# Gate table, gate waits and the order of weight splits in a two-block transformer kernel

## What is computed

```python
# linear attention's gates: two rank-16 projections, log-sigmoid, running sums
la_f = heads(jax.nn.log_sigmoid((zf @ w_gate_f + b_gate_f).astype(F32)) / GLA_TAU, GLA_HK)
la_b = heads(jax.nn.log_sigmoid((zb @ w_gate_b + b_gate_b).astype(F32)) / GLA_TAU, GLA_HK)
b = jnp.cumsum(log_a.astype(F32).reshape(bsz, nh, n, c, dk), axis=3)
q_in = qf * jnp.exp(b)
scores = jnp.einsum('bhncd,bhnjd->bhncj', q_in, kf * jnp.exp(-b))
# differential attention: queries and keys normed and turned by rope, then scores
q, k, v = split_cols(h @ w_in, [D_MODEL, D_MODEL, D_MODEL])
q = rope(rms_norm(q.reshape(bsz, seq, nh, 2, dh), g_q).reshape(bsz, seq, 2 * nh, dh), pos)
k = rope(rms_norm(k.reshape(bsz, seq, nh, 2, dh), g_k).reshape(bsz, seq, 2 * nh, dh), pos)
s = jnp.einsum('bhtqd,bhtkd->bhtqk', q_blk, kt).astype(F32) * scale
# the gated addition at the end of each layer
gate = jax.nn.sigmoid(rms_norm(h, ple_norm[i]) @ ple_w_gate[i])
h = h + gate * (p[i] @ ple_w_proj[i])
```

## Time and profile before

| | us |
|---|---|
| median of three runs (899.43 to 899.6) | 899.53 |
| the profiled execution | 899.7 |
| its span | 897.9 |
| TensorE busy | 892.8 |
| VectorE busy | 653.1 |
| ScalarE busy | 506.9 |
| fetches of units | 295 of 512 KB |

### The profile page before, as it was taken

The page is one execution under the profiler, slowest core; times in us unless marked ns, Lnnn a source line. Parts: engine busy times, 40 slices in busy tenths (PEclk is TensorE's granted clock), DMA queues, the critical chain, the costliest instruction groups (busy, mean ns, idle before and its releaser), DMA issues.

```text
span 897.9 us, 12240 instructions
## 1 busy us (share of the span) xinstructions
PE 892.8 (99%) x4364; PEld 738.6 (82%) x4364; DVE 653.1 (73%) x985; ACT 506.9 (56%) x820; POOL 69.4 (8%) x88
## 2 busy tenths in 40 slices
PE   9999999999999999999999999999999999999998
PEld 8988888888888888778888888888888888887777
DVE  5985478777745688997787777645778997779763
ACT  6756455444444666788664444434665555577681
POOL 0000100000000303211000000000010000215100
PEclk9999999999999999999999999999999999999999
DMA  7674558867755656434387766746567876566621
GB/s 258 205 236 136 179 186 293 283 235 240 247 202 187 226 187 221 143 116 141 127 277 268 244 243 237 253 137 235 197 244 239 286 248 211 191 212 226 222 87 47
DMA packets 76988, 187.47 MB, mean 209 GB/s; under 512 B 6852, under 2 KB 31812, under 8 KB 76936
## 3 DMA queue, kind: packets, MB, share of 16 engines
q1 hardware_dynamic: 75480, 182.99, 59.9%
q0 software_dynamic: 1024, 3.15, 1.0%
q10 hardware_dynamic: 432, 0.66, 0.2%
HBM read 171.83 MB, written 14.94 MB: 208 GB/s over the span
## 4 chain that ended last, share of the span: by engine, by line
PE 98%; DMA 1%; DVE 1%; ACT 0%; issue 0%; DVEq 0%; ACTq 0%
PE bank L1818 86%; PE bank L1856 3%; PE bank L1871 1%; PE bank L2131 1%; PE bank L2157 1%; PE bank L2241 1%; PE bank L2271 1%; DMA h_land<-gate_blocks 1%; PE bank L2142 0%; PE bank L1914 0%; PE bank L1978 0%; PE bank L2227 0%; PE bank L2026 0%; PE bank L2030 0%; PE bank L2251 0%; PE bank L2117 0%
## 5 line engine op out<-in xcount | busy, mean ns | idle before, releaser
L699 ACT ACTIVATE whi<-raw 128x1024 fp32r<-128x1024 f32 x295 | 306.3, 1060 | 181.2 <-DMA raw<-stream_dram 106.2
L1108 DVE TENSOR_TENSOR wlo<-raw,whi 128x1024 fp32r<-128x1024 f32 x295 | 347.9, 1214 | 57.1 <-ACT whi L699 56.7
L1818 PE MATMUL bank<-whi,x_hi 128*128 128x512 f32 x560 | 152.5, 394 | 0.0
L1818 PE MATMUL bank<-wlo,x_hi 128*128 128x512 f32 x560 | 149.9, 390 | 0.0
L1818 PE MATMUL bank<-whi,x_lo 128*128 128x512 f32 x560 | 149.8, 389 | 0.0
L1818 PEld LDWEIGHTS bank<-wlo,x_hi 128*128 128x128 f32 x560 | 105.2, 188 | 22.1
L1818 PEld LDWEIGHTS bank<-whi,x_lo 128*128 128x128 f32 x560 | 105.2, 188 | 21.9
L1818 PEld LDWEIGHTS bank<-whi,x_hi 128*128 128x128 f32 x560 | 103.6, 188 | 22.1 <-issue 1.8
L1818 PE MATMUL bank<-whi,y_hi 128*128 128x512 f32 x396 | 107.8, 394 | 0.6 <-ACT ple_gate L895 0.5
L1818 PE MATMUL bank<-wlo,y_hi 128*128 128x512 f32 x396 | 106.0, 390 | 0.0
L1818 PE MATMUL bank<-whi,y_lo 128*128 128x512 f32 x396 | 106.0, 390 | 0.0
(11 more groups left out here) (252 smaller groups left out, 898.7 us busy)
## 6 DMA issues: line engine op xcount, KB each, us to landing
raw<-stream_dram SPq DMA_DIRECT2D x295, 512.0 KB, 4.6
ffn_blocks<-ffn_blk SPq DMA_DIRECT2D x22, 256.0 KB, 2.0
ffn_land<-ffn_blocks SPq DMA_DIRECT2D x22, 256.0 KB, 4.0
second_blocks<-h_blk SPq DMA_DIRECT2D x8, 256.0 KB, 2.0
h_land<-second_blocks SPq DMA_DIRECT2D x8, 256.0 KB, 2.8
cv_blocks<-cv_blk SPq DMA_DIRECT2D x7, 256.0 KB, 5.0
cv_land<-cv_blocks SPq DMA_DIRECT2D x7, 256.0 KB, 3.1
h_blocks<-h_blk SPq DMA_DIRECT2D x3, 512.0 KB, 6.3
```

Source lines behind the costliest of these rows:

```text
L699: A(whi[:, u % RING, :], raw[:, u % RAW, :], ACT.Copy).then_inc(sem("w_hi"), 1)
L1108: V.tensor_tensor(wlo[:, u % RING, :], raw[:, u % RAW, :], whi[:, u % RING, :].bitcast(F32), ALU.subtract).then_inc(sem("w_lo"), 1)
L1818: last = T.matmul(bank[pair + t][:, :], lhs[a][:, kt, t * P:(t + 1) * P], w[:, u % RING, kk * NW:(kk + 1) * NW], start=part != 1 and k == ...
```

## The change

It has three parts. At each layer's gate, ScalarE takes the sigmoid of one column into a buffer that nobody reads, right behind the squares and ahead of the wait for `rstd`, which loads sigmoid's table there. VectorE waits for the sigmoids of one half of the tokens ahead of each multiplication, where it waited for both ahead of the first. And the tables of order are renumbered: linear attention's `gates` on VectorE go from unit 5 to 4 and `expabs` on ScalarE from 6 to 5; differential attention's first two tiles on ScalarE go from units 4 and 8 to 2 and 6, and VectorE's steps for them two units or one earlier.

```diff
     "act": (
-        (6, "expabs", 0), (7, "ln", 0), (9, "cumulate", 0), (10, "cumulate", 1), (13, "tile", 3), (17, "cross", 0),
+        (5, "expabs", 0), (7, "ln", 0), (9, "cumulate", 0), (10, "cumulate", 1), (13, "tile", 3), (17, "cross", 0),
...
     "dve": (
-        (4, "zT", 0), (4, "tile", 1), (5, "z4", 0), (5, "gates", 0), (7, "ln", 0), (9, "tile", 2),
+        (4, "zT", 0), (4, "tile", 1), (5, "z4", 0), (4, "gates", 0), (7, "ln", 0), (9, "tile", 2),
...
     "act": (
-        (4, "tile", 0), (8, "tile", 1), (11, "qkT", 0), (12, "qkT", 1), (12, "tile", 2), (12, "qkT", 2),
+        (2, "tile", 0), (6, "tile", 1), (11, "qkT", 0), (12, "qkT", 1), (12, "tile", 2), (12, "qkT", 2),
...
     "dve": (
-        (5, "rope", 0), (6, "more", 0), (6, "sums", 0), (8, "rope", 1), (8, "sums", 1), (10, "more", 1),
+        (3, "rope", 0), (4, "more", 0), (4, "sums", 0), (7, "rope", 1), (7, "sums", 1), (10, "more", 1),
...
-        sb("rstd_q", [P, TT])
+        spare = sb("spare", [P, TT])
...
                 squares(j, 1)
+                A(spare[:, n:n + 1], cols[:, 0:1], ACT.Sigmoid)
                 act.wait_ge(sem("rstd"), j + 1)
...
-                    dve.wait_ge(sem("ple_sig"), TT * (2 * n + half + 1))
                     c.wait(dve, "w_used", END[t + 2])
                     for k in range(TT):
+                        dve.wait_ge(sem("ple_sig"), TT * (2 * n + half) + k + 1)
                         V.tensor_tensor(gated[:, k, :], sig[:, k, :], bank[2 * ((t + 1) % 2) + k][:, :], ALU.mult)\
                             .then_inc(sem("ple_gated"), 1)
```

## The result

The changed kernel takes 901.64 us (median of 18 runs, 900.56 to 902.46), the kernel before, run beside it, 899.18 (18 runs, 898.15 to 900.74): a ratio of 1.0027, 95% interval 1.0021 to 1.0033, so 2.5 us or 0.27% slower. The profiled execution of the changed kernel has a span of 900.1 us, that of before 897.9. From line 887 on, lines of the changed kernel stand one higher than before.

What follows compares the result with a forecast made beforehand. TensorE, busy 892.8 of 897.9 us, was taken as the bound. Gates 0, linear attention +1.0 and differential attention +1.6 sum to +2.6: 899.7 + 2.6 = 902.3 us profiled, 902.1 for the median; range 900.2 to 903.6.

Steps and rivals of the forecast that it cites:

- the first part: Whole kernel: TensorE works 892.8 of 897.9 us, so reordering can win only about half a microsecond but can lose more.
- The cover: First gate: VectorE's 3.53 us idling, ended by TensorE's projection, absorbs splits put back 0.1 to 0.7 us; cost nothing.
- So the 0.5 us wait of the earlier trace stays.: Second gate: TensorE still waits 0.5 us for both sigmoids, which stand behind the DMA returning the turned blocks.
- the forecast 328.45: Second gate: VectorE starts the second half's first product one sigmoid earlier, at about 328.45 instead of 328.99.
- One sign: Linear attention: TensorE waits for la at the running sums and for kD at the edge scores; 1.0 us late in all.
- Hidden: Linear attention: unit 10's late low half delays unit 14's fetch, landing at 40.1, but ScalarE takes it only at 41.8.
- the half microsecond that I had set for it in the upper bound: Linear attention, upper bound +1.5: fetches of units 14 to 16 leave together and land half a microsecond late.
- The path: Differential attention: late fetch delays ScalarE's splits and qkT copies, third copy ending 368.55 instead of 366.75; +1.6 us.
- b+13's split: Differential attention, b its first unit: VectorE's split of unit b+13 falls behind tile 1's rope and sums, 357.28 to 358.4.
- the step that I named: VectorE's rope and sums of tile 1, moved ahead of unit b+13's low half, delay b+17's fetch from 353.50 to 358.6.
- Rope and sums of tile 0 come 1.3 us sooner, which nobody waits for: Differential attention on VectorE: tile 0's steps come 1.3 us earlier, with no engine waiting for them.
- each place biting alone: Rival: only one late place costs, linear attention alone 900.5 us or differential attention alone 901.2 us; chance 0.20.

Runs made afterwards that it cites:

- the two kernels with a wait of 2.10 us at the same place: One: only differential attention's tile 1 on ScalarE moved from 8 to 6 against the kernel before, ratio 1.0025; the other is not named outright.
- the run with rope 1 put back: Kernel before with differential attention's tiles moved as in the change, but VectorE's rope and sums of tile 1 left at unit 8: 901.28 us, ratio 1.0027.
- the copies ahead: Kernel before with the change's differential attention order, plus ScalarE's first three qkT copies moved ahead of splits (10, 11, 11): 901.33 us, ratio 1.0031.

## Why the prediction was right, point by point

**The bound.** TensorE's busy time did not change, and its new waits are most of the loss (0.95, 0.58 and 0.57 us in the rows above), as the first part said.

**The gates: 0 predicted, 0.0 measured alone.** The cover held: the splits moved back 0.45 us (308.75 less the 0.31 by which this projection is late, for 307.99), inside the 0.1 to 0.7. One sentence failed: "So the 0.5 us wait of the earlier trace rows stays." It is gone after. But it is also gone in runs without the gate edit and 0.2 in the run with it alone. It goes with the landing of the turned blocks: from VectorE's second transposition to the step of ScalarE that reads the last blocks back it is 7.83 us before, 7.61 and 7.78 in the two other runs with this wait, and 6.79 to 7.55 in the runs without it. So it is no gain of this change. I took one execution's wait for a fixed cost. The second half's multiplication did not start earlier either: it stands at 329.01 for the forecast 328.45, and its row says that it waits for TensorE's projection, no longer for the sigmoid.

The Trainium skill (ScalarE: Activation LUTs, What ACT_TABLE_LOAD costs) adds 1.38 us of draining to a load's 1.28. Here the load took 1.28 and the activation behind it started 0.02 us after it; no run shows the second part, so the row's 1.28 us is what counts here.

**Linear attention: +1.0 predicted, 0.96 in the profile, 1.1 alone.** Each step stands in the rows: the first min in its place with idle time in front, the split between exponentials and table load, no slack behind it. One sign came out smaller than the working had it: at the edge scores, which wait for kD, only 0.10 of the 0.96 is added, since most had been lost at the running sums. What the prediction called "Hidden", the fetch behind unit 10's late half, is hidden only because the exponentials are later still. Alone it costs 0.58, close to the half microsecond that I had set for it in the upper bound. The two don't add.

**Differential attention: +1.6 predicted, 1.76 at the first scores and 1.94 at the later ones, 1.5 alone.** The path came out nearly to the row: fetch at 358.60 for 358.6, split at 361.75 for 361.85, the second at 364.19 for 364.2, the third copy's end at 368.53 for 368.55, the scaling's end at 364.16 for 364.2. What the working lacked is that ScalarE's tile 1 also moved past b+13's split. It costs 2.48 by itself, and undoing the step that I named cures nothing (+2.31 by the yardstick). The size was right because the two overlap, and the fetch ended last. That the move which I had not followed added nothing to it is luck. That "Rope and sums of tile 0 come 1.3 us sooner, which nobody waits for" holds in time, but not as the whole price of tile 0's move: its low halves make b+14 late, and only tile 1's place hides that.

**The sum: 902.1 predicted, 901.64 measured.** The 0.46 between them is partly the kernel before, whose median beside it was 899.18 and not 899.53; the difference is 2.46 for 2.6. Of the rivals, each place biting alone gave 1.1 and 1.5 us, as priced, but both bit.

## What to carry to other kernels

When a step moves past units of an in-order stream, list on every engine the units that change sides, and follow each to the fetch that reuses its buffer; moving two engines together can hide one engine's cost behind the other's, so undoing one of them tells little. If the bound engine has a microsecond of idle time in all, look at a reordering for what it can lose and hardly for what it can win. A wait that one profile shows is a cost only if it recurs in the profiles of kernels that share that place.

## What the runs showed of the hardware that I had not expected

TensorE's granted clock fell during one of its waits. In the run with tile 0 alone moved, TensorE waited 2.81 us ahead of the third transposes, and its timeline goes on:

```profile
365.57 1.09 PE L2117 MATMUL bank<-consts,df_tok 128*128 128x128 f32 x4 [2.81 <-issue]
366.31 2.05 PE L1818 MATMUL bank<-whi,y_hi 128*128 128x512 f32 x4
368.16 1.91 PE L1818 MATMUL bank<-wlo,y_hi 128*128 128x512 f32 x4
```

The table by stretches gives a granted clock of 1.00 up to 364.5 us, 0.77 from there to 365, 0.50 (1.2 of 2.4 GHz) from 365 to 371, and 1.00 from 372 on. So it fell while TensorE still waited, and rose when TensorE had been working again. In the profiles of the two kernels with a wait of 2.10 us at the same place it is 1.00 throughout, and the four matmuls behind the transposes take 1.18 us there, not 2.05. From the transposes' start to the scores it is 6.11 us here and 3.33 in the run with rope 1 put back: 2.8 us of clock on top of 2.8 of waiting, together nearly all of this profile's +5.71 by the second yardstick (71.21).

It does not happen in every execution. Each comes with its mean granted clock. Of this kernel's seven, three have 0.996 or 0.998 and took 902.81 to 904.38 us; the four at 1.00 took 901.15 to 902.51. So part of its ratio of 1.0038 is the clock. Means of 0.998 stand also in one execution each of the two kernels with the 2.10 us wait (902.88 us both) and in three of the eight with the copies ahead, whose longest wait in the profile is 1.53 us (902.40 to 903.78 us). No other kernel here has one below 1.00, and none of those has a wait over 1.2 us. Only one of these executions was profiled, so where the clock fell in the others is not shown.
